# Weight matrices stored so that each partition's share of a load is one contiguous run

## Time and profile before

| | |
|---|---|
| median of the runs | 2658.27 us |
| profiled execution | 2655.39 us, its span 2653.6 us |
| busy: PE, DVE, ACT, POOL | 84%, 43%, 25%, 23% |
| DMA | 864.09 MB in 218552 packets, 326 GB/s over the span |
| of it gathers (queue 0), loads (queue 1) | 536.90 MB, 325.74 MB |

### The profile page before, as it was taken

How to read it: one execution, slowest core, us unless ns; L and a number is a source line. 1 busy time by engine, 2 the same in 40 slices (tenths; PEclk the granted TensorE clock), 3 DMA queues, 4 the chain that set the end, 5 groups by cost and what they waited for, 6 DMA issues and landing times.

```text
span 2653.6 us, 22160 instructions
## 1 busy us (share of the span) xinstructions
PE 2229.6 (84%) x7907; PEld 1067.1 (40%) x7907; DVE 1152.7 (43%) x2829; ACT 655.5 (25%) x1832; POOL 598.7 (23%) x516
## 2 busy tenths in 40 slices
PE   6899999777778888997877777699896799998997
PEld 2454655222223336553323232244454444444443
DVE  1151766565565556675666764400435310000001
ACT  2142333222332322332333332301232110000001
POOL 0000444343433432443444444200000000000000
PEclk8988999899999999999999999899896899999999
DMA  9334899999999987999999999844200479999995
GB/s 347 119 138 156 340 419 419 414 419 414 418 413 417 397 355 275 418 421 416 421 419 407 421 420 421 335 153 157 99 1 0 174 296 394 394 394 395 394 394 222
DMA packets 218552, 864.09 MB, mean 326 GB/s; under 512 B 11180, under 2 KB 18476, under 8 KB 152648
## 3 DMA queue, kind: packets, MB, share of 16 engines
q0 software_dynamic: 73728, 536.90, 49.0%
q1 hardware_dynamic: 144712, 325.74, 32.8%
HBM read 861.55 MB, written 1.05 MB: 325 GB/s over the span
## 4 chain that ended last, share of the span: by engine, by line
PE 43%; DMA 37%; DVE 7%; ACT 5%; issue 3%; POOL 2%; SPq 2%; POOLq 0%; DVEq 0%; ACTq 0%
DMA ring<-in_experts,arena 19%; PE bank L1699 15%; PE bank L1956 14%; DMA arena<-in_w_up 11%; DMA arena<-in_experts,arena 7%; PE bank L2214 5%; PE bank L1708 2%; SPq L615 2%; DVE ring L1252 2%; POOL ring L644 2%; ACT arena L824 2%; PE bank L1756 1%; DVE arena L1252 1%; PE bank L1768 1%; PE bank L1769 1%
## 5 line engine op out<-in xcount | busy, mean ns | idle before, releaser
L1956 PE MATMUL bank<-ring,arena 128*128 128x512 f32 x1024 | 498.8, 633 | 148.7 <-ACT arena L824 148.7
L1956 PE MATMUL bank<-arena 128*128 128x512 f32 x1024 | 487.9, 622 | 111.0 <-ACT arena L824 110.9
L644 POOL DMA_INDIRECT arena<-in_experts,arena x256 | 295.3, 1154 | 716.9 <-PE bank L1956 345.5
L1252 DVE SCALAR_TENSOR_TENSOR ring<-ring,h 128x1024 f32<-128x1024 f32 x256 | 313.8, 1226 | 280.2 <-DMA ring<-in_experts,arena 279.4
L1252 DVE SCALAR_TENSOR_TENSOR arena<-arena,h 128x1024 f32<-128x1024 f32 x256 | 313.6, 1226 | 228.4 <-DMA arena<-in_experts,arena 227.0
L644 POOL DMA_INDIRECT ring<-in_experts,arena x256 | 303.1, 1184 | 373.5 <-PE bank L1956 332.5
L1956 PEld LDWEIGHTS bank<-ring,arena 128*128 128x128 f32 x1024 | 195.0, 200 | 436.5 <-ACT arena L824 232.9
L1956 PEld LDWEIGHTS bank<-arena 128*128 128x128 f32 x1024 | 191.4, 196 | 388.4 <-issue 199.3
L815 ACT ACTIVATE arena<-arena 128x2 f32<-128x2 f32 x256 | 52.1, 203 | 916.3 <-DVE ring L1252 468.2
L2214 PE MATMUL bank<-ring,arena 128*64 128x512 f32 x768 | 233.8, 605 | 29.7 <-DMA arena<-in_w_up 28.4
L1699 PE MATMUL bank<-ring,hT 128*128 128x512 f32 (+2 forms) x640 | 253.4, 558 | 3.0 <-ACT hT L690 2.2
(11 more groups left out here) (393 smaller groups left out, 1835.9 us busy)
## 6 DMA issues: line engine op xcount, KB each, us to landing
ring<-in_w_gate SPq DMA_DIRECT2D x32, 2048.0 KB, 18.1
ring<-in_mod_w SPq DMA_DIRECT2D x24, 2048.0 KB, 24.6
ring<-in_w_up SPq DMA_DIRECT2D x16, 2048.0 KB, 19.2
arena<-in_w_up SPq DMA_DIRECT2D x16, 2048.0 KB, 20.0
ring<-in_w_down SPq DMA_DIRECT2D x16, 2048.0 KB, 14.2
arena<-in_w_down SPq DMA_DIRECT2D x16, 2048.0 KB, 18.9
ring<-in_w_in SPq DMA_DIRECT2D x9, 2048.0 KB, 7.8
ring<-in_peer_w_q SPq DMA_DIRECT2D x8, 2048.0 KB, 13.0
```

The lines of the kernel that those rows point to most:

```text
L644: pool.indirect_dma_start(out=gslot(l, n), out_offset=None, in_=a["experts"], in_offset=bass.IndirectOffsetOnAxis(ap=idx_all[:, t, at:at + ...
L1252: ins = v.scalar_tensor_tensor(out=row, in0=row, scalar=1.0, in1=h[:, t], op0=ALU.mult, op1=ALU.mult, accum_out=act[:, t, HEAD * hh + k:HE ...
L1956: ins = pe.matmul(bank[2 * t + c][:, :], diag[:, PER * (j % 2) + k], row[:, 512 * c:512 * c + 512], start=j % (GROUPS // NT) == 0 and k == ...
```

## The change

The host stores every weight matrix chunk by chunk. Within the array of a matrix, row p holds all that partition p receives: for each chunk in turn its k x n numbers. A load reads `[:, at:at + k * n]` of it, one contiguous run for each partition (16 KB for a 2 MB load). The 32 experts' matrices become `[32, 128, 4096]`. Destination, size, order, slots and waits of all loads stay as they were. The gathers, their table, and the loads of x, constants, biases and gains are not touched.

```diff
+CHUNKS_512 = [(512 * c, 512) for c in range(12)]
+INC = [(512, 512), (0, 512), (1024, 512), (1536, 256)]
+ZC = [(512 * c, min(512, Z_W - 512 * c)) for c in range(10)]
+DEALT = {"mod_w_0": CHUNKS_512, "mod_w_1": CHUNKS_512, "attn_in_w": INC, "attn_out_w": CHUNKS_512[0:2],
+         "peer_w_q_0": CHUNKS_512[0:4], "peer_w_q_1": CHUNKS_512[0:4], "pool_w": [(0, 256)], "w_in_2": ZC,
+         "cmp_w1_k_2": [(0, 256)], "cmp_w1_v_2": [(0, 256)], "w_proj_nsa_2": [(0, D)], "w_proj_gla_2": [(0, D)],
+         "w_out_2": CHUNKS_512[0:2]}
...
-        def kn(w, c0, n):
+        def dealt(name, c, k=KT):
 
-            return w.rearrange("(k p) n -> p k n", p=P)[:, :, c0:c0 + n]
+            chunks = DEALT[name]
+            at = k * sum(n for _, n in chunks[:c])
+            return a[name][:, at:at + k * chunks[c][1]].rearrange("p (k n) -> p k n", k=k)
...
-        stream("mod0", [kn(a["mod_w"][0], 512 * c, 512) for c in range(4)], lambda c: ("modp", mod_part(0, c, 1) + 1))
+        stream("mod0", [dealt("mod_w_0", c) for c in range(4)], lambda c: ("modp", mod_part(0, c, 1) + 1))
...
                 for j, w in enumerate(("w_gate_2", "w_up_2", "w_down_2")):
-                    kk = 8 if j < 2 else 4
                     for k in range(2):
                         if i:
                             sp.wait_ge(S[("moe_g", "moe_u", "moe_y")[j]], 8 * i)
-                        sp.dma_start(w_moe[3 * k + j].rearrange("p (k n) -> p k n", k=kk),
-                                     a[w][2 * i + k].rearrange("(k p) n -> p k n", p=P)).then_inc(moe_landed[3 * k + j], 16)
+                        sp.dma_start(w_moe[3 * k + j], a[w][2 * i + k]).then_inc(moe_landed[3 * k + j], 16)
...
+    def deal(m, chunks):
+
+        m = m.reshape(-1, P, m.shape[-1]).transpose(1, 0, 2)
+        return np.concatenate([m[:, :, c0:c0 + n].reshape(P, -1) for c0, n in chunks], 1)
+
+    def deal_experts(w):
+
+        return np.ascontiguousarray(w.reshape(32, -1, P, w.shape[-1]).transpose(0, 2, 1, 3)).reshape(32, P, SLOT)
```

More of the change, by code:

```diff
@@ L362, in regain @@
             turn[at:at] = lent[l]
-        stream("mod0", [kn(a["mod_w"][0], 512 * c, 512) for c in range(4)], lambda c: ("modp", mod_part(0, c, 1) + 1))
-        INC = [(512, 512), (0, 512), (1024, 512), (1536, 256)]
-        stream("in1", [kn(a["attn_in_w"], c0, n) for c0, n in INC], lambda c: ("pin1", 2 * c + 2))
-        stream("mod0_rest", [kn(a["mod_w"][0], 512 * c, 512) for c in range(4, 12)],
+        stream("mod0", [dealt("mod_w_0", c) for c in range(4)], lambda c: ("modp", mod_part(0, c, 1) + 1))
@@ L368, in program @@
+        stream("in1", [dealt("attn_in_w", c) for c in range(4)], lambda c: ("pin1", 2 * c + 2))
+        stream("mod0_rest", [dealt("mod_w_0", c) for c in range(4, 12)],
                lambda c: ("modp", mod_part(0, 4 + c, 0) + 1))
-        stream("out1", [kn(a["attn_out_w"], 512 * c, 512) for c in range(2)], lambda c: ("pout1", 3 + c))
-        stream("wq0", [kn(a["peer_w_q"][0], 512 * c, 512) for c in range(3)], lambda c: ("pq", query_no(0, 2 * c + 1)))
+        stream("out1", [dealt("attn_out_w", c) for c in range(2)], lambda c: ("pout1", 3 + c))
@@ L371, in program @@
+        stream("wq0", [dealt("peer_w_q_0", c) for c in range(3)], lambda c: ("pq", query_no(0, 2 * c + 1)))
         lend(0)
-        stream("wq0_last", [kn(a["peer_w_q"][0], 512 * c, 512) for c in range(3, 4)], lambda c: ("pq", query_no(0, 7)))
-        stream("mod1", [kn(a["mod_w"][1], 512 * c, 512) for c in range(10)], lambda c: ("modp", mod_part(1, c, 0) + 1))
+        stream("wq0_last", [dealt("peer_w_q_0", c) for c in range(3, 4)], lambda c: ("pq", query_no(0, 7)))
+        stream("mod1", [dealt("mod_w_1", c) for c in range(10)], lambda c: ("modp", mod_part(1, c, 0) + 1))
@@ L374, in program @@
         regain(0, 2)
-        stream("pool", [a["pool_w"].rearrange("g (k p) e -> p (g k) e", p=P)], lambda c: ("py_pool", 4))
-        stream("wq1", [kn(a["peer_w_q"][1], 512 * c, 512) for c in range(3)], lambda c: ("pq", query_no(1, 2 * c + 1)))
+        stream("pool", [dealt("pool_w", 0)], lambda c: ("py_pool", 4))
+        stream("wq1", [dealt("peer_w_q_1", c) for c in range(3)], lambda c: ("pq", query_no(1, 2 * c + 1)))
         lend(1)
-        stream("wq1_last", [kn(a["peer_w_q"][1], 512 * c, 512) for c in range(3, 4)], lambda c: ("pq", query_no(1, 7)))
@@ L379, in program @@
-        stream("mod1_rest", [kn(a["mod_w"][1], 512 * c, 512) for c in range(10, 12)],
+        stream("wq1_last", [dealt("peer_w_q_1", c) for c in range(3, 4)], lambda c: ("pq", query_no(1, 7)))
+        stream("mod1_rest", [dealt("mod_w_1", c) for c in range(10, 12)],
                lambda c: ("modp", mod_part(1, 10 + c, 0) + 1))
-        ZC = [(512 * c, min(512, Z_W - 512 * c)) for c in range(10)]
-        stream("in2", [kn(a["w_in_2"], c0, n) for c0, n in ZC[0:2]], lambda c: ("pin2", 2 * c + 2))
+        stream("in2", [dealt("w_in_2", c) for c in range(2)], lambda c: ("pin2", 2 * c + 2))
@@ L383, in program @@
         regain(1, 0)
[L384 to L388, removed]
@@ L389, in program @@
-        stream("out2", [kn(a["w_out_2"], 512 * c, 512) for c in range(2)], lambda c: ("pout2", 2 * c + 2))
+        stream("in2_rest", [dealt("w_in_2", c) for c in range(2, 10)], lambda c: ("pin2", 2 * c + 6))
+        stream("w1k", [dealt("cmp_w1_k_2", 0, 16)], lambda c: ("hid", 1))
+        stream("w1v", [dealt("cmp_w1_v_2", 0, 16)], lambda c: ("hid", 2))
+        stream("nsa", [dealt("w_proj_nsa_2", 0, 4)], lambda c: ("branch", 4))
+        stream("gla", [dealt("w_proj_gla_2", 0, 4)], lambda c: ("branch", 8))
@@ L391, in query_load @@
+        stream("out2", [dealt("w_out_2", c) for c in range(2)], lambda c: ("pout2", 2 * c + 2))
         def query_load(l, c):
@@ L2325 @@
         pos3[32 * g:32 * g + 15, 2] = pos[31::16]
+    def deal(m, chunks):
[3 more added lines that the diff above has]
+        return np.ascontiguousarray(w.reshape(32, -1, P, w.shape[-1]).transpose(0, 2, 1, 3)).reshape(32, P, SLOT)
+    whole = {"mod_w_0": f["mod_w"][0], "mod_w_1": f["mod_w"][1], "peer_w_q_0": f["peer_w_q"][0], "peer_w_q_1": f["peer_w_q"][1],
+             "pool_w": f["pool_w"][0].reshape(D, 256)}
     arrays = {
         "x": f["x"][0], "ctx": f["ctx"][0], "const": shape_constants(), "cols": np.ascontiguousarray(cols), "rows": rows,
-        "gains": gains, "pos3": pos3, "mod_w": f["mod_w"], "mod_b": f["mod_b"], "attn_in_w": f["attn_in_w"][0],
-        "attn_out_w": f["attn_out_w"][0], "pool_w": f["pool_w"][0], "peer_w_q": f["peer_w_q"],
-        "experts": np.concatenate([f["peer_down"], f["peer_up"]], 2).reshape(2 * EXPERTS, 2 * D), "w_in_2": f["w_in_2"][0],
-        "cmp_w1_k_2": f["cmp_w1_k_2"][0], "cmp_w1_v_2": f["cmp_w1_v_2"][0], "w_proj_nsa_2": f["w_proj_nsa_2"][0],
-        "w_proj_gla_2": f["w_proj_gla_2"][0], "w_out_2": f["w_out_2"][0], "w_gate_2": f["w_gate_2"][0],
-        "w_up_2": f["w_up_2"][0], "w_down_2": f["w_down_2"][0]}
+        "gains": gains, "pos3": pos3, "mod_b": f["mod_b"],
+        "experts": np.concatenate([f["peer_down"], f["peer_up"]], 2).reshape(2 * EXPERTS, 2 * D),
+        "w_gate_2": deal_experts(f["w_gate_2"][0]), "w_up_2": deal_experts(f["w_up_2"][0]),
+        "w_down_2": deal_experts(f["w_down_2"][0])}
+    for name, chunks in DEALT.items():
+        arrays[name] = np.ascontiguousarray(deal(whole[name] if name in whole else f[name][0], chunks))
     nc = bacc.Bacc("TRN2", target_bir_lowering=False, num_devices=1)
```

## The result

The changed kernel takes 2611.57 us (median of 4 runs, 2609.63 to 2613.27), the kernel before on the same chip 2658.49. The ratio is 0.9829, 95% interval 0.9815 to 0.9842: 46.9 us less. I had said 2614.5. The profiled execution's span is 2611.5 us (2653.6 before).

What follows compares the result with a forecast made beforehand. DMA was taken to bound retrieval and, with PE close, the experts. Savings of 36.9 (experts), 6.4 (retrieval) and 0.5 (start) sum to 43.8 us, giving 2614.5 us; its own range was 2609 to 2622, with rivals 2609 to 2637.

Steps and rivals of the forecast that it cites:

- Bounds: Whole kernel: DMA full in retrieval and with the experts, PE close there; cheaper transfers pay there and hardly elsewhere.
- Cost of a packet: All loads: 8.3 ns per packet plus 37.1 ns per 1000 bytes, so 16 KB packets move at 426 GB/s.
- Rival B: 16 KB packets move only at 409 GB/s; DMA stays the experts' bound, 18.5 us saved there; 2636 us; chance 0.14.
- The experts' 36.9 us: Fourteen expert periods fall from 449.5 to 412.6 us: PE's waits and slow matmuls go, PE sets the pace.
- The clock: Experts: with the waits gone, PE runs at full clock and the 8.5 us of slow up matmuls go.
- Rival C: Experts: the clock still falls 5 times, so only 28.4 us saved there; 2623 us; chance 0.10.
- Retrieval's 6.4 us: Retrieval: fourteen loads beside the gathers each save 0.46 us of full engine time, 6.4 in all.
- rival D: Retrieval: 16 KB packets bunch the gathers and DMA idles, 112 us lost against 43.8 gained; 2727 us; chance 0.04.
- The start: Program start: PE's first instruction waits for the first `mod_w` load, which saves 0.5 us.

Runs made afterwards that it cites:

- C: Not a run: stretch of a profiled execution from the first `w_in_2` load to the first `w_gate`; 385.5 us before, 387.3 changed.
- D: Not a run: stretch of a profiled execution from the first `w_gate` to the storing of the output; 557.5 us before, 519.7 changed.
- A: Not a run: stretch from layer 1's first bias load to `pool_w`, bulk of layer 0's retrieval with ten `mod1` loads; 545.4 us before, 538.8 changed.
- B: Not a run: stretch from `pool_w` to the first `w_in_2` load, layer 1 and its retrieval; 712.4 us before, 713.5 changed.
- the pair of halved kernels: Ten `mod1` loads of layer 0's retrieval cut to half, in the changed kernel (2589.23 us) and in the kernel before (2628.71 us).

## Why the prediction was right

Step by step:

- **Bounds.** The experts' stretch by DMA, close above PE; retrieval by DMA: shown by halving bytes in each. Halves gain 25 us in layer 0, 8 in layer 1, and 2.8 with the experts once runs are 16 KB. That the rest is indifferent to loads was not tested so. C, with 16 of those loads, took 385.5 to 388.1 us with them as before and 383.4 to 388.2 with them contiguous.
- **Cost of a packet.** 426 GB/s was forecast for 16 KB, 427 measured. Rival B's 409 GB/s is out as a rate; 4 KB runs have it, and cost 20 us. The 8.3 ns per packet that gave the forecast predicted the 8 KB and 4 KB runs too. By the rule of the Trainium skill (DMA: Bandwidth & Descriptors, Why small descriptors are slow), some 3 bus cycles, going from 4 to 16 KB runs would by estimate have been worth 1.7% (131/128 cycles against 515/512), and it was 4.4% (409 to 427 GB/s).
- **The experts' 36.9 us.** The mechanism was right, and in the execution that the sum was read from the size too: 37.5 us. That is partly luck, for two errors cancel. PE's own period was taken as 29.47 us and is 29.25, so 14 could have taken 409.5, 3.1 less than the forecast 412.6. Nothing was allowed for lateness, yet 2.5 us are left: one wait of 1.0 us, and 29.34 to 29.58 us for most of the later periods. The 0.22 us a period are PE's too: before, gate took 6.87 us and up, behind its wait, 7.10, together 13.97; run through, the two take 13.73. Why is not shown; the first pair took 13.95 in both kernels without a wait for a load. On average D is 39.2 us shorter (559.0, mean of three with the loads as before, 519.8, mean of seven with 16 KB), since the kernel before was read in the mildest of the three: 14 waits and 5 slow groups, where the other two have 15 and 6.
- **The clock.** Rival C, 8.5 us, did not come. The slow groups are in the kernel before (5) and with only the streams contiguous (6), and in none of the three executions of the changed kernel. They are PE at the lower level for a part of the group: over such a one (2325.5 to 2334.3 us) the granted clock is 0.81. With 4 KB runs PE waits 17.9 us in 13 times, and one group, at 2372.53 us, is slow (8.78 us, again at 0.81). It stands behind a wait of 2.6 us; a second wait of 2.6 us, at 2588.95, has a group at full pace behind it, and the other 11 waits, of 1.4 us or less, have too. The 5 slow groups of the kernel before stand behind waits of 2.4 us and more, but so do 4 at full pace. The wait alone does not decide.
- **Retrieval's 6.4 us.** The sum is right by luck: its parts are not. A is 6.4 shorter (545.3 to 538.8, ten kernels with contiguous `mod1`) where ten loads should give 4.6. B, where three should give 1.4, gives 0.2. About 2 us in A do not scale with the bytes of the loads, as the pair of halved kernels shows. Where they lie can be seen, in the share of the 16 engines that each queue's packets took over most of A (535 us from its start before, 529 after):

```profile
q0 software_dynamic: 27272, 198.61, 90.1%
q1 hardware_dynamic: 10856, 22.57, 11.0%
...
q0 software_dynamic: 27330, 199.02, 90.8%
q1 hardware_dynamic: 1896, 22.57, 10.1%
```

  The loads' packets take 53.4 us in place of 58.9, 5.5 less. The gathers' take 480.3 in place of 482.0, though the change does not touch them. Six more executions give the same shares within 0.1%. Why the gathers' packets became cheaper is open.
- **Bursts, rival D.** Packets take turns as forecast. The two queues while loads are in flight, over 14 us each, before (460 to 474) and after (452 to 466):

```profile
q0 software_dynamic: 620, 4.51, 78.2%
q1 hardware_dynamic: 620, 1.27, 23.7%
...
q1 hardware_dynamic: 265, 4.00, 67.2%
q0 software_dynamic: 275, 2.00, 34.5%
```

  As many packets of each, so the loads have 22% of the bytes before and 67% after. A load lands in 12.1 us in place of 28.3 (I had said 10). Gathers are held back meanwhile. Their median landing does not show it (11.6 us in place of 13.8), but DVE's longest wait for one does, 7.1 us in place of 3.0, and their issues do: the 80th gather of layer 0 is issued at about 482 us in place of 478, though the 60th came 0.7 earlier. By the 256th it is 7.3 ahead. PE stands idle longer too, as below. But the DMA share is 1.01 from 448 to 642 us, and the pace is the DMA's.
- **The start.** PE's first wait ends at 12.07 us in place of 12.70, 0.6 less where 0.5 was expected. It can't be followed to the end: the first matmul group took 6.59 us in place of 5.09 in this execution, with a granted clock of 0.96 over the first 45 us. In the two later ones of the same kernel it took 5.48 and 6.03, at 1.00. At the start of A neither it nor the 0.46 us of `wq0_last` can be seen: A starts at 447.1 us on average of three kernels with the loads ahead of it as before, and at 447.0 of eleven with them contiguous, and these lie between 445.5 and 448.8.

## What to carry to other kernels

Where the DMA engines are full, price each packet from two stretches of one's own trace with different run lengths (here 8 ns, and 37 ns per 1000 bytes, on one of 16 engines), and lay weights out so that a partition's share is one run. Then ask what stands next: PE's own time was 8% under the DMA's, so nothing beyond 16 KB runs, not even half the bytes, gave more than 3 us. A layout pays only where transfers bound; 41 of the 151 loads lie elsewhere, and gave nothing that could be seen in the total.

## What the runs showed of the hardware

- A run of 16 KB is moved as one packet: queue 1 makes 24776 packets in all, where the count with 128 for each of the 151 loads gave 24,800, and 16 engines sustain 427 GB/s with them.
- Two queues on the same engines took turns by packet, with 2 KB and with 16 KB against the other's 8 KB (620 to 620 and 265 to 275 packets). Changing one queue's packets from 2 to 16 KB turned the shares round: its loads land in 12.1 us, no longer 28.3, and the other's wait.
- Two issues of a gate load by SyncE took 0.8 us together with 16 KB runs and up to 9.47 us with 2 KB runs, while the DMA engines were full in both.
- Beside such a burst TensorE's clock fell, and no time was lost by it that could be seen. From the first `mod1` load on, the kernel before had 0.94, the changed one 0.77, while the DMA stayed full:

```profile
449.50:478.00 28.50, 19.63 (x46) 8.08 (x44) 18.27 (x60) 7.24 (x26) 11.14 (x10) 0.94 1.02 413
```

```profile
448.80:478.00 29.20, 19.09 (x40) 8.20 (x39) 15.75 (x53) 5.98 (x21) 7.35 (x7) 0.77 1.01 423
```

  PE sat idle 3.79 and 5.59 us in the changed kernel, 2.80 at most before. Behind the 3.79 a group of eight matmuls took 6.21 us in place of 3.70, at a granted clock of 0.50 from 460 to 464 us, the lower level (PE's list, start and us):

```profile
452.65 3.70 PE L1963 MATMUL bank<-arena 128*128 128x512 f32 x8 [0.73 <-ACT arena L831]
460.14 6.21 PE L1963 MATMUL bank<-arena 128*128 128x512 f32 x8 [3.79 <-ACT arena L831]
```

- Stretch C, the same work in all fourteen executions, took 383.4 to 388.2 us, with PE's busy time and granted clock moving along (330.9 us at 0.91, 334.5 at 0.90). Differences of totals under 4 us are better read from the stretch that an edit touches.
